# Prompt attention of a two-layer decoder on one core: the two heads of a pair walked together, value products alternating in the column halves

## The chip, the cores and the metric

One Trainium2 chip; the program runs on one of its cores. The metric is the time of one launch in microseconds (us) of device time. Engines are named as in the profile: PE is TensorE (PEld its weight loads), DVE VectorE, ACT ScalarE, POOL GpSimd, SP SyncE, whose queue only issues transfers here. The profile is of one execution.

## The reference, cut to what matters

One inference step of a decoder trunk with two layers, in fp32: a prompt of 256 tokens and 8 sample tokens, width 1024, 16 heads of 64, an MLP of width 4096 behind each mixer. The change touches the prompt's attention of both layers.

Layer 0 is a dilated sliding-window attention with three groups of keys (window, dilation: (128, 1), (512, 4), (2048, 16)). For each head and query the softmax runs in each group and the outputs are merged by the denominators, which is one softmax over all keys of the three groups:

```python
def mixer_a_prompt(h, w_in, w_out, table):
    ...
        for g, (window, dil) in enumerate(DIL_PATTERNS):
            qb = lax.dynamic_slice_in_dim(qs[g], q0, A_Q_BLOCK, axis=1)
            o, l = dilated_group(qb, ks[g], vs[g], q_idx, window, dil, table)
            outs.append(o)
            lses.append(l)
        return merge_by_denominator(outs, lses)
```

Layer 1 is a sparse attention with three branches (15 compressed keys, selected blocks, a sliding window), each with its own softmax, and their outputs added with sigmoid gates; 16 query heads share 4 key and value heads. A T5 relative bias is added to the logits of every branch in both layers.

## The kernel before

The 256 prompt tokens lie in two query tiles of 128. A unit `u` is one head and one query tile: `h, qt = u // 2, u % 2`, so the order is the small tile of a head (keys 0 to 127), then its big tile (keys 0 to 255), then the next head. There are 32 units in each layer. I call the prompt attention of layer 0 stage a and that of layer 1 stage b.

A unit of stage a passes through these steps, each on its engine, joined by semaphores:

- PE, `score_a` (L655 to L664): three products (one for each group of keys) of the queries with the keys, 64 rows deep, since a head has 64 values. The 64 rows are the lower or the upper half of the partitions by the head's parity. One fp32 product is two matmul instructions in the profile. The results lie in bank 0 (small) or banks 1 and 2 (big).
- DVE, `logits_a` (L1209 to L1224): scale, plus a mix of bias and mask, which POOL makes once a head (L540 to L547) in one of two buffers, `mixes[h % 2]`. The mix of head h waits until the logits of the units up to 2h-3 are read.
- DVE, `max_a` (L1226): maximum. ACT, `exp_a` (L1699): exponential with its sum. DVE, `diag_of` (L1195 to L1201): a diagonal matrix with the reciprocal of the sum, waiting for ACT's sum.
- PE, `turn_probs` (L699 to L710): the probabilities, in pieces of 128 columns, times the diagonal, which turns and normalises them: 3 pieces in a small unit, 6 in a big one. Results in bank 3 (small) or 4 and 5 (big). ACT, `pt_a` (L1745 to L1751) copies them out into one of two buffers, `PT`.
- PE, `pv_a` (L712 to L721): value products, 64 columns of weights each, in one column half of bank 6 or 7, 3 or 6 of them. DVE, `evac_o` (L1188): evicts the 64 x 128 result.

The orders are written out by hand. PE's loop (L732 to L745) issues for each u: scores of u+2, turn of u, value products of u-1. DVE's (L1267 to L1285): logits of u, diagonal of u-1, maximum of u, eviction of u-3, and at u = 5 and 9 a merge of the samples' outputs, `mix_a` (L1206 and L1207). ACT's: exponential of u, copy of u-1. Behind the last head's mix POOL adds the last mask to the whole bias (L549), loads a table and adds two weights (L554).

Stage b has the same shape (`score_b` L892, `pv_b` L951, PE's loop L966; `logits_b` L1394, `max_b` L1408, `rc_of` L1385, DVE's loop L1484; ACT's loop L1835). A unit has one product over 15 compressed keys and two over 128 or 256; its three sums are handled together, and POOL makes the three diagonals (L561 to L568), which wait for `rc_of`. Turned pieces: 1 of 15 rows and 2 or 4 of 128. Value products: L959 (15 rows) and L962.

SyncE's queue carries weights (L500), copies of the caches to the outputs (L452) and, between the two, the loads of layer 1's pages: `cmp_loads` (L402 to L414), which for the first sample waits for the last logits of stage a. POOL issues its own `cmp_loads` behind L554. Layer 1's projection in front of stage b (`tile`, banks 0 and 1, the last ones 7 and 6) issues the first scores between its last tiles.

## Time and profile before

| | us |
|---|---|
| median of 3 runs | 1675.91 |
| lowest, highest | 1675.38, 1677.29 |
| the profiled execution's own time | 1680.73 |
| its span | 1679.0 |
| stage a in it | 376.7 to 507.7 |
| stage b in it | 1131.1 to 1241.8 |

The mean clock that was granted to PE in this execution is 0.964 of full speed. The profiled execution stood 0.29% over the median. A group in the timeline is a run of instructions of one line on one engine: when it started, how long it was busy, the line, the operation, output and inputs, the count, and in brackets the idle time before it with what ended that. Its busy time has the end of the last instruction in it, so groups on PE overlap by some 0.1 us, and start to start is the measure of a period. A few matmul records can be missing, so that a count is 11 where 12 ran.

### The profile page before, as it was taken

How to read it: one execution, taken by the hardware profiler on the slowest of the kernel's cores; microseconds unless marked ns; L12 is line 12 of the kernel's file. 1: busy time of each engine (PE TensorE's matmuls, PEld its weight loads, DVE VectorE, ACT ScalarE, POOL GpSimd, SP SyncE). 2: the span in 40 equal slices, each digit the busy share in tenths (PEclk: the TensorE clock that was granted, in tenths of full speed). 3: DMA queues.
4: the chain of work that ended last, by engine and by line, in shares of the span. 5: the costliest groups of instructions: out<-in, count | busy, mean ns of one | idle time of the engine just before them, and what ended most of it. 6: DMA issues, size and time to landing. Idle time of an engine off the chain costs nothing.

```text
span 1679.0 us, 23479 instructions
## 1 busy us (share of the span) xinstructions
PE 1579.3 (94%) x8609; PEld 1279.6 (76%) x8609; DVE 663.4 (40%) x1533; ACT 387.4 (23%) x1166; POOL 203.4 (12%) x301
## 2 busy tenths in 40 slices
PE   6999998999989999999999999999997778999998
PEld 5877787766878878887888887886764446888886
DVE  2246512118872321003576674326546552322001
ACT  1011111113431000002566663115533220000000
POOL 1100000012230200001111120005532320000000
PEclk8799999999999999999999999999989898999999
DMA  5499999999959998787799991419966877998740
GB/s 183 158 356 383 410 401 360 337 373 355 330 164 249 284 363 299 272 292 135 128 140 140 149 186 38 122 61 352 343 200 220 285 266 242 386 372 304 276 146 31
DMA packets 170979, 423.34 MB, mean 252 GB/s; under 512 B 10400, under 2 KB 131560, under 8 KB 168064
## 3 DMA queue, kind: packets, MB, share of 16 engines
q1 hardware_dynamic: 147840, 344.27, 62.6%
q0 software_dynamic: 19312, 67.47, 15.1%
q10 hardware_dynamic: 3728, 10.32, 1.7%
q8 instruction: 58, 0.95, 0.3%
q14 instruction: 41, 0.34, 0.1%
HBM read 413.88 MB, written 192.48 MB: 361 GB/s over the span
## 4 chain that ended last, share of the span: by engine, by line
PE 82%; DMA 7%; DVE 7%; issue 2%; ACT 1%; SPq 1%; POOL 0%; ACTq 0%; DVEq 0%; POOLq 0%
PE bank L626 21%; PE bank L801 14%; PE bank L787 12%; PE bank L708 4%; PE bank L878 3%; PE bank L881 3%; PE bank L830 3%; PE bank L883 3%; DMA a_win_sample<-oT 2%; PE bank L719 2%; PE bank L663 2%; PE bank L756 1%; DMA cring<-cache_b_kv 1%; PE bank L1041 1%; DMA wring<-mlp_w_up 1%
## 5 line engine op out<-in xcount | busy, mean ns | idle before, releaser
L626 PE MATMUL bank<-hT,wring 128*128 128x264 f32 (+1 forms) x1488 | 354.0, 393 | 0.5 <-DVE area L1359 0.5
L626 PEld LDWEIGHTS bank<-hT,wring 128*128 128x128 f32 (+1 forms) x1488 | 279.2, 192 | 67.2 <-issue 8.2
L787 PE MATMUL bank<-hT,wring 128*128 128x264 f32 x1024 | 230.1, 388 | 1.9 <-DMA wring<-mlp_w_up 1.9
L801 PE MATMUL bank<-area,wring 128*128 128x264 f32 x1024 | 229.2, 386 | 2.8 <-DVE area L1312 2.8
L787 PEld LDWEIGHTS bank<-hT,wring 128*128 128x128 f32 x1024 | 195.6, 191 | 36.1 <-issue 2.3
L801 PEld LDWEIGHTS bank<-area,wring 128*128 128x128 f32 x1024 | 194.1, 190 | 37.2 <-DVE area L1310 3.6
L1689 ACT ACTIVATE turned<-xT 128x264 f32<-128x264 f32 x40 | 16.9, 423 | 548.1 <-DVE xT L1316 463.1
L1316 DVE TENSOR_TENSOR xT<-bank,xT 128x264 f32<-128x264 f32 x16 | 6.9, 432 | 224.6 <-PE bank L801 224.6
L1310 DVE SCALAR_TENSOR_TENSOR area<-bank,rv 128x264 f32 x64 | 27.7, 432 | 163.0 <-PE bank L787 162.3
L567 POOL TENSOR_SCALAR area<-ident,small 128x128 f32<-128x128 f32 x96 | 56.3, 603 | 179.4 <-DVE small L1392 179.4
L1242 DVE TENSOR_TENSOR area<-bank,rv 128x264 f32<-128x264 f32 x48 | 20.8, 432 | 106.0 <-PE bank L626 106.0
L626 PE MATMUL bank<-oT,wring 128*128 128x264 f32 x256 | 61.5, 398 | 0.9 <-DVE oT L1656 0.5
L529 POOL DMA_DIRECT2D cring<-cache_a_win x24 | 17.6, 734 | 339.4 <-PE bank L651 154.5
L626 PEld LDWEIGHTS bank<-oT,wring 128*128 128x128 f32 x256 | 50.1, 197 | 10.3 <-DVE oT L1656 0.8
L414 POOL DMA_DIRECT2D area<-cache_b_kv x32 | 17.0, 531 | 282.6 <-issue 282.6
L1242 DVE TENSOR_TENSOR oT<-bank,rv 128x264 f32<-128x264 f32 x24 | 10.4, 432 | 92.5 <-PE bank L626 92.5
L708 PE MATMUL bank<-hT,turned 128*128 128x128 f32 x240 | 36.4, 304 | 9.1 <-DVE hT L1201 8.8
L708 PE MATMUL bank<-area,turned 128*128 128x128 f32 (+1 forms) x256 | 39.9, 287 | 4.7 <-POOL area L567 3.2
L708 PEld LDWEIGHTS bank<-hT,turned 128*128 128x128 f32 x240 | 31.8, 209 | 15.6 <-issue 15.3
L708 PEld LDWEIGHTS bank<-area,turned 128*128 128x128 f32 (+1 forms) x256 | 27.6, 166 | 19.4 <-issue 18.4
L1840 ACT ACTIVATE turned<-turned,small 128x15 f32<-128x15 f32 (+2 forms) x96 | 37.8, 395 | 19.4 <-DVE small L1418 19.4
L1201 DVE SCALAR_TENSOR_TENSOR hT<-ident,small 128x128 f32<-128x128 f32 x32 | 39.8, 1244 | 1.1
(325 smaller groups left out, 2330.7 us busy)
## 6 DMA issues: line engine op xcount, KB each, us to landing
a_win_sample<-cache_a_win SPq DMA_DIRECT2D x64, 2047.0 KB, 19.5
wring<-a_w_in SPq DMA_DIRECT2D x36, 1024.0 KB, 13.0
wring<-mlp_w_up SPq DMA_DIRECT2D x32, 1024.0 KB, 10.8
wring<-mlp_w_down SPq DMA_DIRECT2D x32, 1024.0 KB, 5.3
a_win_sample<-cache_a_win SPq DMA_DIRECT2D x16, 2044.0 KB, 19.0
cring<-cache_a_win POOLq DMA_DIRECT2D x24, 1024.0 KB, 11.9
cring<-cache_b_kv POOLq DMA_DIRECT2D x62, 256.0 KB, 6.3
cring<-cache_b_kv SPq DMA_DIRECT2D x50, 256.0 KB, 7.7
```

The costliest lines, as they stand in the source:

```text
L567: ins = nc.gpsimd.tensor_scalar(diag_b[:, u % 2, k, :], ident[:, :], rc2[:, 3 * (u % 4) + k:3 * (u % 4) + k + 1], None, ALU.mult)
L626: mm = pe.matmul(bk[half if bank is None else bank][0:width, 0:R], wring[:, blk % NW, c, half * P:half * P + width], rhs[:, c, :], start=( ...
L663: mm = pe.matmul(out, qT[q0:q0 + HD, g, c, qt * P:(qt + 1) * P], kT[q0:q0 + HD, g, c, 0:n], start=True, stop=True)
L708: mm = pe.matmul(b[0:w, (j % 4) * P:(j % 4 + 1) * P], src[:, at_:at_ + w], diags[j], start=True, stop=True)
L787: mm = pe.matmul(bk[half][:, 0:R], wring[:, blk % NW, c, half * P:(half + 1) * P], hT[:, c, :], start=(c == 0), stop=(c == DC - 1))
L801: mm = pe.matmul(bk[half][:, 0:R], wring[:, blk % NW, c, half * P:(half + 1) * P], upT[:, f * R:(f + 1) * R], start=(f == 0), stop=(f == F ...
L830: mm = pe.transpose(bk[2 + h][:, i * P:(i + 1) * P], src[:, h, 2 * v + i // 2, k, (i % 2) * P:(i % 2 + 1) * P], ident[:, :])
L878: pe.matmul(accs[1][:, 0:256], wab[:, k, v + 4 * f, :], x[:, f, 1], start=(v + f == 0), stop=(v + f == 4))
L881: pe.matmul(accs[0][:, 0:256], w1[:, k, 0, v + 4 * f, :], d1[:, f], start=(v + f == 0), stop=(v + f == 4))
L883: mm = pe.matmul(accs[2][:, 0:252], w1[:, k, 1, v + 4 * f, :], d2[:, f, :, 0:63], start=(v + f == 0), stop=(v + f == 4))
L1201: dve.scalar_tensor_tensor(diag_a[:, u % 2, :], ident[:, :], rc2[:, u % 4:u % 4 + 1], ident[:, :], ALU.mult, ALU.mult).then_inc(S["diag_re ...
L1840: ins = nc.scalar.activation(L[:, a:a + w], L[:, a:a + w], ACT.Exp, bias=mx2[:, o + k:o + k + 1], accum_out=sm2[:, o + k:o + k + 1])
```

## The change

Both prompt attentions walk the heads in pairs. The order of units is now small tile of the even head, small tile of the odd head, big tile of the even, big tile of the odd (`unit(u)`). Scores get one of four places (`score_banks`). The value products run once for each pair and tile, `pv_a(w)` and `pv_b(w)`: the products of the two heads alternate, each in its column half of bank 7. One eviction of 128 x 128 takes both. So PE's loop issues value products at every second u, u even, for the two units u-2 and u-1.

Buffers follow: four mixes and four buffers for the turned probabilities where there were two of each. The mixes of heads 4 and up wait for the logits of the pair two before. The turned pieces of the small units lie in banks 3 and 4 by parity, the fifth and sixth piece of a big unit in bank 5, in its left half for the even head and in its right half for the odd; the latter waits for the copy of the unit before. The copy of a unit waits for the value products of two pairs and tiles before. The first `cmp_loads` wait for the last value products of stage a instead of its last logits. The wait for `rows_evac` 71 in front of the first scores is gone, and the wait for `oa_copied` stands in front of the scores of unit 3. The last tiles of layer 1's projection lie in banks 7 and 5.

```diff
--- before.py
+++ after.py
@@ -188,7 +188,7 @@
-        mixes = (cring[:, 0, 2048:2816], cring[:, 0, 3072:3840])
+        mixes = (cring[:, 0, 2048:2816], cring[:, 0, 3072:3840], cring[:, 1, 2304:3072], cring[:, 1, 3072:3840])
...
@@ -204,8 +204,8 @@
-        LG = (turned_f[:, 1536:1920], turned_f[:, 0:768], small[:, 128:512], turned_f[:, 768:1536])
-        PT = hT_f[:, 0:2 * 768].rearrange("p (i n) -> p i n", i=2)
+        LG = (turned_f[:, 1536:1920], small[:, 128:512], turned_f[:, 0:768], turned_f[:, 768:1536])
+        PT = (cring[:, 1, 0:384], cring[:, 1, 384:768], cring[:, 1, 768:1536], cring[:, 1, 1536:2304])
...
@@ -251,10 +251,10 @@
-        PB = hT_f[:, 0:2 * 640].rearrange("p (i n) -> p i n", i=2)
+        PB = (hT_f[:, 0:384], hT_f[:, 384:768], hT_f[:, 768:1408], hT_f[:, 1408:2048])
...
-        LB = (turned_f[:, 0:272], turned_f[:, 544:1072], turned_f[:, 272:544], turned_f[:, 1072:1600])
+        LB = (turned_f[:, 0:272], turned_f[:, 272:544], turned_f[:, 544:1072], turned_f[:, 1072:1600])
...
@@ -303,6 +303,14 @@
+        def unit(u):
+            return 2 * (u // 4) + u % 2, u // 2 % 2
+        def score_banks(u):
+            return ((bk[0], None), (bk[1], None), (bk[2], bk[0]), (bk[1], bk[6]))[u % 4]
         def a_slot(i):
...
@@ -402,7 +410,7 @@
         def cmp_loads(eng, b, js, landed_sem):
...
-                eng.wait_ge(S["logits_read"], 2 * H)
+                eng.wait_ge(S["pv_done"], 2 * H)
...
@@ -541,9 +549,11 @@
                     for i in range(NA, 2 * NK):
...
-                if h >= 2:
-                    pool.wait_ge(S["logits_read"], 2 * h - 2)
-                nc.gpsimd.tensor_tensor(mixes[h % 2].rearrange("p (g k) -> p g k", g=NG), bias[:, h, :].unsqueeze(1).broadcast_to([P, NG, 2 * P]),
+                if h in (2, 3):
+                    pool.wait_ge(S["pva_done"], 12)
+                if h >= 4:
+                    pool.wait_ge(S["logits_read"], 4 * (h // 2 - 2) + 3 + h % 2)
+                nc.gpsimd.tensor_tensor(mixes[h % 4].rearrange("p (g k) -> p g k", g=NG), bias[:, h, :].unsqueeze(1).broadcast_to([P, NG, 2 * P]),
...
@@ -653,13 +663,14 @@
             def score_a(u):
-                h, qt = u // 2, u % 2
+                h, qt = unit(u)
...
+                b, b2 = score_banks(u)
                 for g in range(NG):
-                    out = bk[0][:, g * P:(g + 1) * P] if qt == 0 else (bk[1][:, g * 256:(g + 1) * 256] if g < 2 else bk[2][:, 0:256])
+                    out = b[:, g * n:(g + 1) * n] if g < 2 or qt == 0 else b2[:, 0:256]
...
@@ -702,25 +713,28 @@
                     pe.wait_ge(S["pt_ready"], u[0] - 1)
                 pe.wait_ge(S["probs_ready"], u[0] + 1)
                 pe.wait_ge(S["diag_ready"], u[0] + 1)
-                at_ = 0
+                at_, e = 0, u[1] % 2
                 for j, w in enumerate(widths):
-                    b = bk[3] if u[1] % 2 == 0 else bk[4 + j // 4]
-                    mm = pe.matmul(b[0:w, (j % 4) * P:(j % 4 + 1) * P], src[:, at_:at_ + w], diags[j], start=True, stop=True)
+                    if j == 4 and e:
+                        pe.wait_ge(S["pt_ready"], u[0])
+                    b, o = (bk[3 + e], j * P) if j < 4 else (bk[5], 256 * e + (j - 4) * P)
+                    mm = pe.matmul(b[0:w, o:o + P], src[:, at_:at_ + w], diags[j], start=True, stop=True)
                     at_ += max(w, 16)
                 mm.then_inc(S["probs_turned"], 1)
-            def pv_a(u):
-                h, qt = u // 2, u % 2
-                pe.wait_ge(S["pt_ready"], u + 1)
-                if u >= 2:
-                    pe.wait_ge(S["o_evac"], u - 1)
-                n, e = qt + 1, h % 2
+            def pv_a(w):
+                c, qt = w // 2, w % 2
+                pe.wait_ge(S["pt_ready"], 2 * w + 2)
+                if w:
+                    pe.wait_ge(S["o_evac"], 2 * w)
+                n = qt + 1
                 for j in range(NG * n):
-                    mm = pe.matmul(bk[6 + u % 2][64 * e:64 * e + 64, 0:P], V[:, j % n, j // n, h * HD:(h + 1) * HD], PT[:, u % 2, j * P:(j + 1) * P],
-                                   start=(j == 0), stop=(j == NG * n - 1))
-                mm.then_inc(S["pv_done"], 1)
-            pe.wait_ge(S["rows_evac"], 71)
+                    for e in range(2):
+                        h = 2 * c + e
+                        mm = pe.matmul(bk[7][64 * e:64 * e + 64, 0:P], V[:, j % n, j // n, h * HD:(h + 1) * HD], PT[2 * qt + e][:, j * P:(j + 1) * P],
+                                       start=(j == 0), stop=(j == NG * n - 1))
+                mm.then_inc(S["pv_done"], 2)
             score_a(1)
             pe.wait_ge(S["rows_evac"], 72)
             for i in range(2 * NS):
@@ -730,19 +744,20 @@
             for u in range(2 * H):
+                if u == 1:
+                    pe.wait_ge(S["oa_copied"], 1)
...
-                n = NG * (u % 2 + 1)
-                if u == 1:
-                    pe.wait_ge(S["oa_copied"], 1)
+                n = NG * (unit(u)[1] + 1)
...
-                if u:
-                    pv_a(u - 1)
+                if u and u % 2 == 0:
+                    pv_a(u // 2 - 1)
...
+            pe.wait_ge(S["pt_ready"], 2 * H - 1)
             for st in range(NS):
...
-            pv_a(2 * H - 1)
+            pv_a(H - 1)
             def turn(n):
...
@@ -915,7 +931,7 @@
-                    tile(blk, half, E_BIN + p, hT, P if j != 6 else 48, p % 2 if p < 19 else 26 - p).then_inc(S["gemm_done"], 1 if j != 6 else 2)
+                    tile(blk, half, E_BIN + p, hT, P if j != 6 else 48, p % 2 if p < 19 else 45 - 2 * p).then_inc(S["gemm_done"], 1 if j != 6 else 2)
...
@@ -948,29 +964,29 @@
             pe.wait_ge(S["gates_ready"], 2)
-            def pv_b(u):
-                h, qt = u // 2, u % 2
-                g, n = h // KVH, qt + 1
-                pe.wait_ge(S["pt_ready"], U0 + u + 1)
-                if u >= 2:
-                    pe.wait_ge(S["o_evac"], U0 + u - 1)
-                e = h % 2
-                o, pt = bk[6 + u % 2][64 * e:64 * e + 64, 0:P], PB[:, u % 2, :]
-                pe.matmul(o, vcP[0:CMP, g * HD:(g + 1) * HD], pt[0:CMP, 0:P], start=True, stop=False)
+            def pv_b(w):
+                c, qt = w // 2, w % 2
+                g, n = c // 2, qt + 1
+                pe.wait_ge(S["pt_ready"], U0 + 2 * w + 2)
+                if w:
+                    pe.wait_ge(S["o_evac"], U0 + 2 * w)
+                for e in range(2):
+                    pe.matmul(bk[7][64 * e:64 * e + 64, 0:P], vcP[0:CMP, g * HD:(g + 1) * HD], PB[2 * qt + e][0:CMP, 0:P], start=True, stop=False)
                 for k in range(2):
                     for j in range(n):
-                        mm = pe.matmul(o, kvrow[:, j, (3 + 2 * k) * GW + g * HD:(3 + 2 * k) * GW + (g + 1) * HD],
-                                       pt[:, (1 + k * n + j) * P:(2 + k * n + j) * P], start=False, stop=(k == 1 and j == n - 1))
-                mm.then_inc(S["pv_done"], 1)
+                        for e in range(2):
+                            mm = pe.matmul(bk[7][64 * e:64 * e + 64, 0:P], kvrow[:, j, (3 + 2 * k) * GW + g * HD:(3 + 2 * k) * GW + (g + 1) * HD],
+                                           PB[2 * qt + e][:, (1 + k * n + j) * P:(2 + k * n + j) * P], start=False, stop=(k == 1 and j == n - 1))
+                mm.then_inc(S["pv_done"], 2)
             for u in range(2 * H):
                 if 4 <= u + 2 < 2 * H:
                     score_b(u + 2)
-                n = u % 2 + 1
+                n = unit(u)[1] + 1
                 turn_probs((U0 + u, u), [CMP] + [P] * (2 * n), LB[u % 4], [diag_b[:, u % 2, 0, :]] + [diag_b[:, u % 2, 1, :]] * n + [diag_b[:, u % 2, 2, :]] * n)
-                if u:
-                    pv_b(u - 1)
-            pv_b(2 * H - 1)
+                if u and u % 2 == 0:
+                    pv_b(u // 2 - 1)
+            pv_b(H - 1)
             pe.wait_ge(S["o_evac"], 4 * H)
@@ -1185,12 +1201,10 @@
-            def evac_o(first, u):
-                h, qt = u // 2, u % 2
-                e = h % 2
-                dve.wait_ge(S["pv_done"], first + u + 1)
-                dve.tensor_copy(oT[64 * e:64 * e + 64, h // 2, qt * P:(qt + 1) * P], bk[6 + u % 2][64 * e:64 * e + 64, 0:P]).then_inc(S["o_evac"], 1)
+            def evac_o(first, w):
+                dve.wait_ge(S["pv_done"], first + 2 * w + 2)
+                dve.tensor_copy(oT[:, w // 2, w % 2 * P:(w % 2 + 1) * P], bk[7][:, 0:P]).then_inc(S["o_evac"], 2)
             def diag_of(u):
...
@@ -1269,20 +1284,19 @@
-                if u >= 3:
-                    evac_o(0, u - 3)
+                if u >= 4 and u % 2 == 0:
+                    evac_o(0, u // 2 - 2)
...
-            evac_o(0, 2 * H - 3)
-            evac_o(0, 2 * H - 2)
+            evac_o(0, H - 2)
...
             for st in range(NS):
                 for e in range(2):
...
-            evac_o(0, 2 * H - 1)
+            evac_o(0, H - 1)
             def square(n):
...
@@ -1429,7 +1444,7 @@
-                src = bk[i % 2 if i < 19 else 26 - i][:, 0:R]
+                src = bk[i % 2 if i < 19 else 45 - 2 * i][:, 0:R]
...
@@ -1742,16 +1757,15 @@
-            def copy_pt(u, parts_cols, PTb):
+            def pt_a(u):
+                e = u % 2
+                parts = [(3 + e, 0, 384, 0)] if u // 2 % 2 == 0 else [(3 + e, 0, 512, 0), (5, 256 * e, 256, 512)]
...
-                if u >= 2:
-                    act.wait_ge(S["pv_done"], u - 1)
-                for parts, bank, c0, n, o in parts_cols:
-                    ins = nc.scalar.copy(PTb[0:parts, o:o + n], bk[bank][0:parts, c0:c0 + n])
+                if u >= 4:
+                    act.wait_ge(S["pv_done"], 2 * (u // 2 - 1))
+                for bank, c0, n, o in parts:
+                    ins = nc.scalar.copy(PT[u % 4][:, o:o + n], bk[bank][:, c0:c0 + n])
...
-            def pt_a(u):
-                copy_pt(u, [(P, 3, 0, 384, 0)] if u % 2 == 0 else [(P, 4, 0, 512, 0), (P, 5, 0, 256, 512)], PT[:, u % 2, :])
             for u in range(2 * H):
...
@@ -1823,18 +1837,19 @@
             def pt_b(u):
-                parts = ([(CMP, 3, 0, P, 0), (P, 3, P, 256, P)] if u % 2 == 0 else
-                         [(CMP, 4, 0, P, 0), (P, 4, P, 384, P), (P, 5, 0, P, 512)])
+                e = u % 2
+                parts = ([(CMP, 3 + e, 0, P, 0), (P, 3 + e, P, 256, P)] if u // 2 % 2 == 0 else
+                         [(CMP, 3 + e, 0, P, 0), (P, 3 + e, P, 384, P), (P, 5, 256 * e, P, 512)])
...
-                if u >= 2:
-                    act.wait_ge(S["pv_done"], U0 + u - 1)
+                if u >= 4:
+                    act.wait_ge(S["pv_done"], U0 + 2 * (u // 2 - 1))
                 for np_, bank, c0, n, o in parts:
-                    ins = nc.scalar.copy(PB[0:np_, u % 2, o:o + n], bk[bank][0:np_, c0:c0 + n])
+                    ins = nc.scalar.copy(PB[u % 4][0:np_, o:o + n], bk[bank][0:np_, c0:c0 + n])
...
             for u in range(2 * H):
...
-                n = (u % 2 + 1) * P
+                n = (u // 2 % 2 + 1) * P
...
                 for k, (a, w) in enumerate(((0, CMP), (16, n), (16 + n, n))):
...
```

## Rows read from the trace of the kernel before

**Rows 1.** The page, part 1: busy time of each engine.

```profile
PE 1579.3 (94%) x8609; PEld 1279.6 (76%) x8609; DVE 663.4 (40%) x1533; ACT 387.4 (23%) x1166; POOL 203.4 (12%) x301
```

**Rows 2.** Windows: length, busy PE, PEld, DVE, ACT, POOL, granted clock, DMA share, GB/s.

```profile
376.70:507.70 131.00, 121.20 (x797) 98.71 (x796) 103.21 (x182) 49.44 (x116) 34.74 (x16) 0.95 0.86 279
1131.10:1241.80 110.70, 106.00 (x682) 76.49 (x682) 62.21 (x278) 58.08 (x260) 52.81 (x90) 1.00 0.96 323
426.00:440.20 14.20, 14.10 (x98) 11.72 (x97) 11.35 (x22) 5.51 (x14) 3.62 (x2) 1.00 1.04 338
1176.60:1190.50 13.90, 13.73 (x90) 9.93 (x89) 8.11 (x36) 7.60 (x34) 7.04 (x12) 1.00 0.98 355
```

**Rows 3.** Timeline of a steady head of stage a, PE, DVE and POOL.

```profile
438.68 1.52 PE L719 MATMUL bank<-hT,area 128*64 128x128 f32 x12
...
440.13 1.56 PE L663 MATMUL bank<-area 64*128 64x256 f32 x6
...
441.62 1.60 PE L708 MATMUL bank<-hT,turned 128*128 128x128 f32 x12
...
442.83 1.82 POOL L546 TENSOR_TENSOR cring<-bias,mprompt 128x768 f32<-128x768 f32 x1 [5.28 <-DVE turned L1223]
442.85 1.94 DVE L1201 SCALAR_TENSOR_TENSOR hT<-ident,small 128x128 f32<-128x128 f32 x1
...
443.15 0.87 PE L719 MATMUL bank<-hT,area 128*64 128x128 f32 x6
...
443.95 0.93 PE L663 MATMUL bank<-area 64*128 64x128 f32 x6
...
444.94 0.91 PE L708 MATMUL bank<-hT,turned 128*128 128x128 f32 x6
```

**Rows 4.** Timeline of a big unit of stage b, PE, DVE and POOL.

```profile
1181.29 0.39 PE L899 MATMUL bank<-area 64*128 64x15 f32 x2
...
1182.57 1.48 PE L708 MATMUL bank<-area,turned 128*15 128x128 f32 x10
...
1184.02 1.76 POOL L567 TENSOR_SCALAR area<-ident,small 128x128 f32<-128x128 f32 x3 [2.27 <-DVE small L1392]
...
1185.93 1.02 PE L708 MATMUL bank<-area,turned 128*15 128x128 f32 x6
```

**Rows 5.** Timeline, PE: products in two column halves, and full-width ones.

```profile
817.63 0.65 PE L839 MATMUL bank<-oT,area 128*64 128x254 f32 x4
...
1004.08 1.03 PE L881 MATMUL bank<-turned,area 128*128 128x256 f32 x4
```

**Rows 6.** Timeline and windows: pauses of PE, and the granted clock around them.

```profile
397.19 1.23 DVE L1206 TENSOR_TENSOR cring<-cring,cb 128x1024 f32<-128x1024 f32 x1
...
398.45 1.90 DVE L1207 TENSOR_REDUCE area<-cring 128x64 f32<-128x1024 f32 x1
...
401.54 2.57 PE L708 MATMUL bank<-hT,turned 128*128 128x128 f32 x12 [1.57 <-DVE hT L1201]
...
489.32 2.90 PE L708 MATMUL bank<-hT,turned 128*128 128x128 f32 x12 [5.06 <-DVE hT L1201]
...
659.58 2.71 PE L801 MATMUL bank<-area,wring 128*128 128x264 f32 x11 [1.39 <-DVE area L1312]
...
401.90:405.30 3.40, 3.40 (x17) 3.06 (x16) 3.33 (x6) 1.56 (x4) 1.81 (x1) 0.50 1.00 344
655.50:659.50 4.00, 2.69 (x13) 1.94 (x11) 1.05 (x3) 0.00 (x0) 0.00 (x0) 1.00 0.83 331
```

**Rows 7.** Timeline: the second turn of stage b.

```profile
1136.47 1.02 PE L708 MATMUL bank<-area,turned 128*15 128x128 f32 x6 [1.03 <-POOL area L567]
```

**Rows 8.** Windows: a stretch behind stage b.

```profile
1250.50:1255.50 5.00, 5.00 (x21) 3.54 (x14) 0.00 (x0) 0.89 (x2) 0.00 (x0) 0.50 0.02 4
```

**Rows 9.** Timeline of SyncE's queue behind stage a; waits from 507 to 700.

```profile
500.72 10.08 SPq L414 DMA_DIRECT2D cring<-cache_b_kv  x8
...
PE bank L787 <- DMA wring<-mlp_w_up: 1.9, 1, 1.9
```

41 lines of the change are left out of this document (22 added, 19 removed).

## The prediction

> **What bounds the kernel now.** I began with the busy table: TensorE (PE) is busy 94% of the span [rows 1], at a mean granted clock of 0.964. Read alone, that says that PE work taken out is time taken out. The change touches two stages, so I went on to the windows: layer 0's prompt attention (stage a) takes 131.0 us and layer 1's (stage b) 110.7 [rows 2]. One steady pair of heads keeps PE busy 14.10 of 14.20 us in a and 13.73 of 13.90 in b [rows 2]. That looks PE-bound, but the timeline shows a tie. In a, PE's groups follow each other start to start as big scores 1.49, big turn (L708, x12) 1.53, small value products (L719) 0.80, small scores 0.96, small turn 0.84, big value products 1.45: 7.07 a head [rows 3]. Beside it runs a loop of waits of the same length: scores 1.56, logits on VectorE (DVE) that bring the diagonal to 442.85, and the diagonal, 1.94 instead of 0.35, because GpSimd's (POOL's) mix of 1.82 starts with it, released by the same logits [rows 3]; then the small turn that needs the diagonal. From the big scores' start to the small turn's are 4.8 us, and 0.84 + 1.45 more close the head. Stage b has the same shape: 6.97 a head, half of the window of a pair (scores 1.28 from row to row, and 0.99, turns 1.41 and 0.98, value products 0.93 and 1.38), with POOL making the diagonals in 1.76 each [rows 4]; from the big scores' start (1181.29, with the compressed keys) to the turn that waits for what they led to (1185.93) are 4.64 us.
>
> **The value products.** A pair's two heads had a run of products each, now they alternate between column halves. The trace has one group of that form: L839, four matmuls of 254 columns in 0.65 us, against 1.03 for four of 256 columns in full width at L881 [rows 5]. So two halves stream beside each other. I cost a pair's run as one head's now: 0.80 + 1.45 saved a pair in a, 0.93 + 1.38 in b, 2.3 us each. Bounds: nothing saved at all, or this.
>
> The Trainium skill, page "TensorE: Matmul & The Clock Gate", section "The mechanism", says that a weight load overlaps running matmuls only where the row groups differ. Here all share the same 128 rows, and by that rule each load would be bare. The trace is against it: L719's twelve loads and matmuls take 1.52 us [rows 3], with nothing left over for bare loads. It is kept as a rival below.
>
> **What takes the place of that work.** The new order is small, small, big, big for each pair. I follow stage a's chain at full clock from one first big turn to the next: 0.13 + big turn 1.53, small products 0.80, small scores 0.96, second big turn 1.53, big scores 1.60; then DVE alone: logits 0.93, diagonal 2.05 (still beside a mix, since both mixes of a pair are now released by the logits of its big units), max 0.95, eviction 0.27, logits 0.93, diagonal 2.05. That is 13.73 us a pair against 14.20, though PE has only 2 x (1.49 + 1.53 + 0.96 + 0.84) + 2.25 = 11.89 of work. The rest, 1.84 us, is a pause in front of the first big turn of a pair: there PE has scores, a small turn and scores (3.29) to do while that turn's diagonal is 5.13 us off. Eight pairs save some 4 us; DVE's two extra merges (L1206 and L1207, 1.23 + 1.90 [rows 6]) now fall partly in the pauses and cost about 1.6 each instead of 3.1, 3 more. At full clock, stage a would give 7.3 us back.
>
> Stage b at full clock: PE work of a pair is 2 x 6.97 - 2.31 = 11.63. The first big turn comes 4.64 us after the second big scores start (2.73 to the diagonals' start, 1.76 of them, 0.15 of hand-over [rows 4]), and only 1.28 + 0.98 + 0.96 of work lies between: a pause of 1.42, and one of 0.28 ahead of the small turn (its diagonals, by the same steps from the small scores). 13.33 a pair against 13.94, some 5 us over the stage. At its start it is worse: the turn at 1136.47 waited 1.03 us for POOL [rows 7]. In the new order it is a big turn, released no earlier, and the small value products (0.93) now come behind it, a big turn ahead has become a small one (0.43), and a hand-over of some 0.3 is gone as well: about 2.7 us of pause.
>
> **The clock.** The change trades a PE that never stops for one that stops in every pair. What the trace shows of that [rows 6]: after the pause of 1.57 us that ended at 401.54, the stretch from 401.9 to 405.3 ran at granted 0.50, the lower level of 1.2 GHz. After 5.06 us in front of 489.32 the same twelve turns took 2.90 instead of 1.60. In 655.5 to 659.5 there was a pause of 1.39 (ended at 659.58) and the clock stayed at 1.00 (2.4 GHz), as it did around the 1.03 in stage b [rows 7, 2]. The new pauses of 1.84 are longer than one that was followed by half clock; that of 2.7 far longer. So I take the clock as lost in a after some five of eight pauses, and surely at the start of b.
>
> Its price in a: 3.40 us of solid work at half clock [rows 6] is 1.7 us of work lost, five or six times, some 9.3. Stage a: -7.3 + 9.3 = **+2**. It comes back there, as it did after 405.3 in before: full-height work is dense.
>
> In b, does it come back? There a score group feeds 64 rows, compressed products 15. The nearest row is L1006's neighbourhood: PE busy 5.00 of 5.00 us with 8-row products, and granted 0.50 throughout [rows 8]. Busy time alone doesn't bring the clock back. I take b between these: once lost it stays lost. Price: the twelve matmuls of L708 went from 1.60 [rows 3] to 2.90 [rows 6], 0.108 us more for each 128 columns. A pair of b streams 32 such in turns, 24 in scores (256 columns counting twice), and 16 in value products: 72 x 0.108 = 7.8, 19.4 us a pair. It is then bound by PE; the pauses vanish. From the first big turn at about 1136.8 to the last pair's are 7 x 19.4 = 135.8, 1272.6; two turns of 2.48, products of 1.57 and 2.45 and the eviction, 9.4: 1282.0, where before came to 1241.8. Stage b: **+40**.
>
> **The rest.** The first page loads of layer 1's cache on SyncE's queue (10.08 us of issue at 500.72 [rows 9]) wait for the last value product instead of the last logits, some 7 us later relative to it. Behind them lie weight loads; PE's one wait on these, 1.9 us [rows 9], may grow by 0 to 2: +0.5. Bank 5, shared by the two big units, makes the odd one's fifth piece wait for the copy of the even one (0.86 at the longest): PE has other groups of some 3 us between the two turns, 0; without that cover 0.86 a pair. Mixes in four buffers: released by the same kind of logits, 0. The eviction for both heads moves 128 partitions instead of 64 in the same 0.27: 16 of 32 go in each stage, off the path. The second projection's bank order, the small scores' banks and the removed wait at the start of a: 0. Copies of turned probabilities wait for value products two units older: covered, 0.
>
> **Sum.** +2 + 40 + 0.5 = +42.5 on the profiled execution's 1680.7 is 1723.2; it stood 4.8 (0.29%) over the median of 1675.9, so **1718** for the median. A measurement of this kernel tells about 0.2%, 3.4 us, from no change.
>
> **The rivals.**
> - Forecast, b at half clock throughout: 1700 to 1727 (with a between -4 and +8, and b's pair 18.5 to 19.8). Chance 0.56.
> - The clock comes back in b between pauses: each pair pays one to two stretches of 1.7 and gains 0.61, 8 x (1.7 to 3.4) - 5 = +9 to +22, with a's +2: 1684 to 1700. For it: stage a in before did come back. 0.15.
> - The clock holds, the other side: pauses of 1.84 leave it at 2.4 GHz in both stages. -7.3 - 5 + 1 = 1665, **faster**. It decides in front of the first big turn of b, at 1136.8: granted 1.00 behind it, and b ends before 1240. For it: 1.39 was borne. Against it: 1.57 wasn't. 0.15. The Trainium skill's same page, section "Why this matters for your kernels", warns only of idle gaps longer than any of these; by that rule the new pauses are harmless and 1665 comes out. The trace disagrees, with the half clock behind 1.57 us.
> - The chain is shorter than I think and PE alone counts: 2.3 a pair in both stages, 16 pairs, 1638. Against: 5.13 from rows. 0.03.
> - The halves don't stream together: a pair in a is 13.73 + 0.80, in b about 15.1, with few pauses left: +2.6 - 3 + 9 = 1684. Against: L839. 0.04.
> - Weight loads stay bare between alternating halves: at most 0.33 a run in a and 0.9 a pair in b: 1675 with the clock held, 1730 with it lost. 0.04.
> - The later loads hold up the MLP's weights just enough to meet the gain, with the clock held: 1673 to 1679. 0.03.
>
> Range: 1668 to 1730; what it leaves out is the clock held (0.15) and PE alone (0.03). Faster by over 0.2%: these two, 0.18. Within: the late loads and half of the bare ones, 0.05. Slower: the rest, 0.77.
>
> **What would show it.** Right: L719 and L962 as groups of x24 and x12 with twice as many matmuls in the same 1.4 to 1.5 us; one pause of 1.8 a pair in a before the first big turn; granted clock of b near 0.5 and its pairs 19 us apart. Wrong: granted 1.00 throughout b (then b is 5 us shorter); value runs of 2.5 us (no overlap); the diagonal at 0.35 in big units (the mix not beside it); PE's wait for MLP weights over 4 us.

## The result, and the profile after

The changed kernel took 1730.21 us (median of 4 runs, 1714.69 to 1738.99), against 1675.64 for the kernel before beside it: a ratio of 1.0325, 95% interval 1.0243 to 1.0408, slower. The forecast was 1718, range 1668 to 1730. The direction and the mechanism came as forecast; stage b's part of it was a quarter larger, and the median lies 0.2 us above the range. Some executions come out longer than the rest, 31 of the 77 of the kernel before that ran beside the experiments, all but one of them by 20 to 80 us, and the ratios leave out, of every kernel, what lies over 1.5% above its fastest execution, while medians count all.

The profiled execution took 1727.76 us, with a span of 1726.0, 47.0 over the one before. The page's busy and clock lines [rows 1]:

```profile
PE 1616.7 (94%) x8609; PEld 1302.7 (75%) x8609; DVE 648.5 (38%) x1501; ACT 385.4 (22%) x1166; POOL 203.4 (12%) x301
...
PEclk8899999998899999998999999965558898999999
```

PE is busy for the same share, with the same number of instructions, and 37 us longer. The clock line has three slices of 5 and one of 6 where it had three of 9 and one of 8. The windows (length, busy PE, PEld, DVE, ACT, POOL, granted clock, DMA share, GB/s) of stage a, of stage b and of one pair of b [rows 2]:

```profile
384.50:504.80 120.30, 102.25 (x753) 85.19 (x752) 92.48 (x162) 46.77 (x112) 31.09 (x14) 0.89 0.83 275
1126.10:1287.60 161.50, 155.78 (x682) 110.26 (x682) 57.42 (x261) 56.87 (x260) 52.81 (x90) 0.52 0.65 221
1152.33:1173.08 20.75, 20.72 (x88) 14.70 (x89) 7.55 (x34) 7.38 (x35) 7.04 (x12) 0.50 0.98 320
```

A pair of b is 20.75 us of unbroken PE work at 0.50. From its first turn to the product behind it, b takes 161.5 us where it took 110.6 (1131.20 to 1241.77 before). The whole account: stage a ends at 504.81 instead of 507.73, -2.9; the stretch between a and b is 2.2 shorter; b +50.9; what lies behind b +1.2. Together 47.0.

The timeline of PE around b's start [rows 7], of the same kernel, and of one pair:

```profile
1126.08 2.00 PE L721 MATMUL bank<-area,turned 128*15 128x128 f32 x12 [0.52 <-DVE area L1449]
...
1131.57 2.59 PE L721 MATMUL bank<-area,turned 128*15 128x128 f32 x10 [2.63 <-POOL area L577]
...
1152.33 2.59 PE L721 MATMUL bank<-area,turned 128*15 128x128 f32 x10
1154.85 0.69 PE L974 MATMUL bank<-hT,area 15*64 15x128 f32 x4
1155.47 1.12 PE L978 MATMUL bank<-hT,area 128*64 128x128 f32 x8
1156.52 0.61 PE L915 MATMUL bank<-area 64*128 64x15 f32 x2
1156.97 1.20 PE L917 MATMUL bank<-area 64*128 64x128 f32 x4
1158.10 2.61 PE L721 MATMUL bank<-area,turned 128*15 128x128 f32 x10
1160.64 0.61 PE L915 MATMUL bank<-area 64*128 64x15 f32 x2
1161.09 2.05 PE L917 MATMUL bank<-area 64*128 64x256 f32 x4
1163.07 1.76 PE L721 MATMUL bank<-area,turned 128*15 128x128 f32 x6
...
1276.85 2.59 PE L721 MATMUL bank<-area,turned 128*15 128x128 f32 x10 [1.60 <-POOL area L577]
```

The pause of 2.63 us stands where it was forecast with 2.7, and the first ten turns behind it take 2.59 instead of 1.48 [rows 4]. Then no group waits until the last pair, whose first big turn waits 1.60 us (1276.85) and whose last value products wait 0.87. In stage a the same view shows a value run for both heads (L734) and then, for five of the eight pairs, the pause in front of the first big turn and what followed it:

```profile
403.04 1.53 PE L734 MATMUL bank<-cring,area 128*64 128x128 f32 x24
...
409.51 1.58 PE L721 MATMUL bank<-hT,turned 128*128 128x128 f32 x12 [1.72 <-DVE hT L1215]
...
424.50 2.49 PE L721 MATMUL bank<-hT,turned 128*128 128x128 f32 x12 [2.25 <-DVE hT L1215]
...
439.62 1.58 PE L721 MATMUL bank<-hT,turned 128*128 128x128 f32 x12 [1.72 <-DVE hT L1215]
...
453.14 1.58 PE L721 MATMUL bank<-hT,turned 128*128 128x128 f32 x12 [1.72 <-DVE hT L1215]
...
466.68 2.90 PE L721 MATMUL bank<-hT,turned 128*128 128x128 f32 x12 [1.72 <-DVE hT L1215]
```

Pairs are 13.5 us apart (439.62, 453.14, 466.68), against 14.2 before. The pause was 1.72 us four times; three times the twelve turns behind it took 1.58 us (full clock) and once 2.90 (half), so the length of a pause doesn't say which.

### The profile page after: what moved, and what is told of

It is laid out like the page before. It is cut to its first block, busy times and chain, and to the rows that moved or that the text cites. A ratio compares the mean times of both kernels' runs of the same rounds, so it can differ in the third digit from the quotient of the medians.

```text
span 1726.0 us, 23447 instructions
## 1 busy us (share of the span) xinstructions
PE 1616.7 (94%) x8609; PEld 1302.7 (75%) x8609; DVE 648.5 (38%) x1501; ACT 385.4 (22%) x1166; POOL 203.4 (12%) x301
## 4 chain that ended last, share of the span: by engine, by line
PE 84%; DVE 7%; DMA 5%; issue 2%; ACT 1%; SPq 0%; POOL 0%; ACTq 0%; DVEq 0%; POOLq 0%
PE bank L636 21%; PE bank L816 13%; PE bank L802 12%; PE bank L721 5%; PE bank L893 3%; PE bank L896 3%; PE bank L845 3%; PE bank L898 3%; PE bank L917 2%; DMA a_win_sample<-oT 2%; DMA wring<-mlp_w_up 1%; PE bank L771 1%; PE bank L1057 1%; PE bank L978 1%; DMA a_win_sample<-area 1%
## 5 line engine op out<-in xcount | busy, mean ns | idle before, releaser
L721 PE MATMUL bank<-area,turned 128*128 128x128 f32 (+1 forms) x256 | 68.3, 430 | 4.9 <-POOL area L577 4.2
L721 PEld LDWEIGHTS bank<-area,turned 128*128 128x128 f32 (+1 forms) x256 | 46.6, 266 | 31.2 <-issue 30.2
L917 PE MATMUL bank<-area 64*128 64x256 f32 (+1 forms) x128 | 47.3, 527 | 0.0
L1847 ACT COPY hT<-bank 15x128 f32<-15x128 f32 (+2 forms) x80 | 20.8, 316 | 106.6 <-PE bank L721 106.6
```

Of the source, the lines that this page charges most:

```text
L721: mm = pe.matmul(b[0:w, o:o + P], src[:, at_:at_ + w], diags[j], start=True, stop=True)
L917: mm = pe.matmul(b[:, o + k * n:o + (k + 1) * n], q, kD[q0:q0 + HD, k, g, 0:n], start=True, stop=True)
```

## The experiments

In all kernels that fill pauses, the filler is this function, whose products nobody reads:

```diff
+            def fill(n):
+                for _ in range(n):
+                    pe.matmul(bk[2][:, 0:P], ident[:, :], ident[:, :], start=True, stop=True)
```

In each comparison the median in brackets is that of all executions of the kernel before beside it; "b" is stage b from its first turn to the product behind it, in the traced execution.

**Is it the pause at b's start, the pauses in its pairs, or the halves?** Four kernels on one chip (before: 1684.15).

```diff
                 n = unit(u)[1] + 1
+                if u == 2:
+                    fill(12)
                 turn_probs((U0 + u, u), ...
```

> The changed kernel, with twelve products of the identity with itself (full height, 128 columns, into bank 2, read by nobody) put into the pause of 2.63 us in front of stage b's first big turn, and nowhere else. Theory (the pause at the start loses the clock and b's light work never wins it back): granted clock of b near 1.00, pairs of 13.3 us with pauses of 1.4 in place of 20.75, b some 50 us shorter, the whole near 1680. Second theory (b's new mix of work with 1.4 us pauses loses the clock again by itself): the clock holds for one or more pairs, then 0.5 for the rest; the whole 1690 to 1720. Rival (the alternating halves, not the pauses, pull the clock down): 0.5 from the first value products on, the whole stays near 1730.

1720.76 us, ratio 1.0265 (1.0201 to 1.0329). Windows of b, first the start, then the stretch up to 1182, then the rest:

```profile
1132.70:1145.00 12.30, 11.65 (x86) 9.15 (x86) 7.27 (x36) 6.71 (x31) 4.54 (x8) 1.00 1.15 417
1145.00:1155.00 10.00, 7.64 (x48) 5.51 (x49) 4.47 (x20) 4.39 (x20) 4.26 (x8) 0.83 0.99 321
1155.00:1182.00 27.00, 23.39 (x178) 16.95 (x178) 15.53 (x72) 15.01 (x68) 14.09 (x25) 0.97 0.96 315
1182.00:1274.00 92.00, 89.44 (x396) 63.55 (x395) 29.98 (x134) 31.09 (x142) 29.91 (x51) 0.50 0.60 206
```

The second theory's case: the start is borne, the clock dips behind a pause of 1.51 us at 1145.9, comes back, bears two pauses of 1.47 (at 1154.4 and 1167.7), and goes behind a third of 1.47, at 1181, until the end of b. b takes 142.0 us in this trace, so the start pause alone isn't the whole of it. The halves run at 1.00 for 12 us, so they don't pull it down.

```diff
+                if u % 4 == 2:
+                    fill(12 if u == 2 else 6)
                 turn_probs((U0 + u, u), ...
```

> As the run before it, and six such products in front of the first big turn of every pair of stage b (1.3 us, as long as the pause). Theory: the clock is 1.00 through all of b, its pair 13.3 us, the whole near 1680. If the pauses of 1.4 matter, this run is faster than the one that fills only the start; if they don't, the same within 3 us. Rival (alternating halves): near 1730 or above, since the fillers then cost 2.6 us a pair at half clock.

1676.45, ratio 1.0008 (0.9967 to 1.0048): 44 us less than with the start alone, for six products a pair that fill the pause. One dip of some 10 us was left, from 1142 to 1152, and b took 111.8 us.

```diff
                 n = NG * (unit(u)[1] + 1)
+                if u > 2 and u % 4 == 2:
+                    fill(8)
                 turn_probs((u, u), ...
```

> As the run before it, and eight such products (1.7 us) in front of each pair's first big turn in stage a too. Theory: no half clock in a but behind the mask's 8.8 us addition, 2 to 3 windows of half clock saved at 1.5 us each: 3 to 5 us faster than the run before it, near 1676. Rival (in a the DVE chain hides what the half clock costs): the same within 2 us.

1671.44, ratio 0.9974 (0.9940 to 1.0008). In its trace b is at 1.00 from end to end and takes 107.1 us, its pairs 13.30 apart (1177.23, 1190.53), which is the full-clock sum of the forecast (13.33):

```profile
1130.50:1237.50 107.00, 100.76 (x788) 76.12 (x788) 57.55 (x261) 57.69 (x260) 52.82 (x90) 1.00 0.98 334
...
1178.64 0.44 PE L981 MATMUL bank<-hT,area 15*64 15x128 f32 x4
1179.00 0.66 PE L985 MATMUL bank<-hT,area 128*64 128x128 f32 x8
1179.59 0.39 PE L922 MATMUL bank<-area 64*128 64x15 f32 x2
```

A small value run for both heads takes 0.95 us start to start at full clock (1178.64 to 1179.59), against the 0.93 of one head before. Stage a took 122.15 us here and between 119.9 and 126.8 in the five traces whose stage a is the change's own, so this run can't tell what the filling of a is worth.

The fourth kernel takes back the alternation alone:

```diff
-                for j in range(NG * n):
-                    for e in range(2):
+                for e in range(2):
+                    for j in range(NG * n):
...
```

> The changed kernel with the alternation alone undone: in each value run the products of the even head come first, then those of the odd head, in the same two column halves, with the same order of units, buffers and single eviction. That puts back 2.3 us of PE work a pair. Theory (pauses lose the clock): in a the pair is 14.5 us, the pause in front of the first big turn stays near 1.8 since none of the work lies there; in b the start pause of 2.6 stays, so b still goes to half clock and takes 2.3 to 4.6 us more a pair: the whole 1750 to 1770. Rival (alternating halves pull the clock down): b at 1.00, 1685 or less. Second rival (the halves don't stream beside each other, so that the order is indifferent): same as the changed kernel, 1730.

1759.19, ratio 1.0486 (1.0403 to 1.0569), as the theory had it: b 186.7 us at a mean clock of 0.56, 25 more than with alternation. A pair of b at half clock, and a big value run of a at full clock, all with the halves in turn:

```profile
447.30 2.46 PE L734 MATMUL bank<-cring,area 128*64 128x128 f32 x24
...
1142.36 2.59 PE L721 MATMUL bank<-area,turned 128*15 128x128 f32 x10 [2.63 <-POOL area L577]
...
1156.44 0.69 PE L974 MATMUL bank<-hT,area 15*64 15x128 f32 x2
...
1161.47 0.61 PE L915 MATMUL bank<-area 64*128 64x15 f32 x2
...
1167.26 2.59 PE L721 MATMUL bank<-area,turned 128*15 128x128 f32 x10
```

The pair takes 24.90 us (1142.36 to 1167.26) where it took 20.75, and the big value run 5.03 (1156.44 to 1161.47) where it took 2.53. So the halves do stream beside each other when they alternate, at half clock too. In a the same 24 matmuls take 2.46 us in turn and 1.53 alternated; a small run takes 1.07 in turn (start to start), less than the 2 x 0.80 of two separate runs before. So in a some of the 2.25 us that a pair saves comes from joining the two heads' runs, and the alternation itself is worth 1.20; in b it is worth the whole 2.3.

**Shorter chains in place of fillers, and the old kernel with a pause.** Four kernels (before: 1681.90).

```diff
-                dve.tensor_tensor(rc, rc, grow[:, qt, h, :], ALU.mult).then_inc(S["rc_ready"], 1)
+                link(dve.tensor_tensor(rc, rc, grow[:, qt, h, :], ALU.mult))
...
+                dve.tensor_tensor(diag_b[:, u % 2], ident[:, :].unsqueeze(1).broadcast_to([P, 3, P]), rc.unsqueeze(2).broadcast_to([P, 3, P]), ALU.mult)...
```

> The changed kernel, with stage b's three diagonals of a unit made by one VectorE instruction (identity times the three reciprocals, 128 x 384) right behind the reciprocals, in place of three GpSimd instructions of 1.76 us together. No filler. An estimate from DVE's rows of that size: 0.4 to 0.6 us. Theory (pauses of over about 1.5 us in a row of light work lose the clock): the start pause falls from 2.63 to some 1.3 and the pause in each pair from 1.4 to near 0, the clock holds at 1.00, a pair takes 11.7 to 12.5 us in place of 13.3: b about 95 to 102 us, the whole 1663 to 1672. Rival (the start pause is still too long): b at half clock, DVE faster or not: 1725 to 1731, since b is bound by PE there.

(The loop of three GpSimd instructions is taken out.) 1701.44, ratio 1.0131 (1.0041 to 1.0221): neither. The diagonals take 0.56 us, and the pauses shrink (1.37 at the start), but b alternates between the levels (1.00 in 1161 to 1179 and 1231 to 1250, 0.50 in 1141 to 1155 and 1186 to 1224) and takes 126.8.

```diff
-                dve.scalar_tensor_tensor(diag_a[:, u % 2, :], ident[:, :], rc2[:, u % 4:u % 4 + 1], ident[:, :], ALU.mult, ALU.mult)...
+                nc.scalar.mul(diag_a[:, u % 2, :], ident[:, :], rc2[:, u % 4:u % 4 + 1]).then_inc(S["diag_ready"], 1)
```

> As the run before it, and stage a's diagonals made on ScalarE (identity times the reciprocal) instead of VectorE, so that no diagonal stands beside a GpSimd mix. Theory: the pause in front of the first big turn of a pair in a goes from 1.84 to 0.1 to 0.5, a's pair from 13.7 to 12.0 to 12.4 us, no half clock in a: 12 to 20 us less than the run before it if the clock holds in b in both. Rival (ScalarE takes the place of the diagonal in the chain, or VectorE's other instructions now collide with the mix): a gains less than 5 us.

1680.65 with runs from 1657.87 to 1702.02, ratio 0.9930 (0.9863 to 0.9997). Stage a, which took 125.1 us before and 120.3 after, takes 95.0:

```profile
385.60:480.60 95.00, 91.63 (x753) 76.04 (x753) 58.05 (x129) 55.96 (x141) 31.28 (x14) 1.00 1.01 339
1099.60:1243.70 144.10, 137.98 (x680) 98.14 (x680) 74.42 (x290) 57.40 (x260) 0.00 (x0) 0.60 0.73 248
...
444.83 1.83 POOL L556 TENSOR_TENSOR cring<-bias,mprompt 128x768 f32<-128x768 f32 x1 [6.28 <-DVE turned L1229]
444.97 0.40 ACT L1769 ACTIVATE hT<-ident,small 128x128 f32<-128x128 f32 x1
```

The diagonal takes 0.40 us on ScalarE beside a mix of 1.83 that made it 1.94 on VectorE [rows 3]. But b is still at 0.60 on average. The clock goes behind the second of two pauses of 1.37 and 1.31 us at its start, and from 1130 to 1170 PE is busy without a pause and stays at 0.50:

```profile
1111.32 1.18 PE L715 MATMUL bank<-area,turned 128*15 128x128 f32 x6 [1.31 <-DVE area L1400]
```

The ratio counts only the five shortest of its ten executions; the medians of all, 1680.65 against 1681.90, show no gain from stage a's 25 us, since b gives them back (144.2 us in this trace).

```diff
--- before.py
+                if u == 2:
+                    for k in range(3):
+                        nc.gpsimd.tensor_scalar(diag_b[:, 0, k, :], ident[:, :], 0.0, None, ALU.mult)...
...
                 for k in range(3):
```

> The kernel before, with nothing of the change in it: three more GpSimd instructions of 0.6 us, writing zeros to a diagonal's buffer that is overwritten at once, in front of the diagonals of unit 2 of stage b. They lengthen the pause that PE has at 1136.5 from 1.03 to about 2.9 us, once. Theory (a pause of that length at the start of b loses the clock, and b's work never wins it back, whatever the order or the halves): granted clock 0.5 through the rest of b, b some 60 us longer, the whole 1730 to 1745. Rival (the order of units or the halves are needed for the loss): b 1.9 us longer, the whole 1676 to 1690.

1696.70 (1678.67 to 1731.18), too scattered for a ratio. Its trace shows both theory and rival short of the mark:

```profile
1135.06 1.02 PE L712 MATMUL bank<-area,turned 128*15 128x128 f32 x6 [2.66 <-POOL area L571]
...
1128.20:1136.00 7.80, 5.14 (x34) 3.65 (x34) 3.65 (x16) 3.65 (x17) 4.38 (x8) 1.00 1.13 405
1138.00:1162.00 24.00, 24.00 (x86) 16.69 (x85) 9.63 (x45) 6.78 (x32) 6.97 (x12) 0.50 1.00 325
1165.00:1250.00 85.00, 82.56 (x532) 59.72 (x531) 47.54 (x210) 45.19 (x201) 42.45 (x72) 1.00 0.81 272
```

The clock went behind the longer pause in the old order too; there it came back after 24 us, and b took 123.7 us, 13 more than before.

```diff
+                if u == 2:
+                    fill(6)
```

> As the run with both diagonals moved, and six filler products (1.3 us) in front of the first big turn of stage b, once. If the start pause of some 1.3 us did no harm without them: the same within 2 us. If the run without them is at half clock in b, this one is 50 us faster: near 1650 to 1660.

1687.63 (1663.81 to 1705.24), ratio 1.0021 (0.9975 to 1.0067), against 1680.65 without: no gain from filling the start pause once the chains are short. The second pause, 1.31 us at 1111.5, was left, and b was at 0.50 for some 60 us from there on.

**Fillers and short chains together, and what belongs to which.** Four kernels (before: 1681.09).

```diff
+                if u % 4 == 2:
+                    fill(12 if u == 2 else 6)
```

> The kernel with both diagonals moved (a's to ScalarE, b's to one VectorE instruction), with twelve filler products in front of stage b's first big turn and six in front of the first big turn of each later pair. Theory (the fillers are what kept the clock in the kernel with all pauses of b filled): b at 1.00 throughout, its pair 12.8 to 13.2 us, b 103 to 108 us, a 95 us as in the run without fillers: the whole 1635 to 1645, faster than the kernel before and than every run so far. Rival (the clock falls in b anyway, since there are fewer pauses to fill and the work is light): b 125 or more, 1660 or above.

1649.73, ratio 0.9843 (0.9781 to 0.9904). b at 1.00 up to its last products, 104.7 us.

```diff
-                    fill(12 if u == 2 else 6)
+                    fill(12 if u == 2 else 3)
```

> The same with three fillers a pair in b instead of six. Theory: if half as much dense work is enough, b's pair is 12.3 us, 4 to 5 us faster than with six. If it isn't, b goes to half clock for some pairs, and this run is 10 to 40 us slower than with six, with a wider scatter from run to run.

1646.31 (1641.26 to 1649.82), ratio 0.9821 (0.9760 to 0.9881), the fastest kernel of the study, though the interval overlaps that of the one with six; its four runs lie within 8.6 us. Stage a and b of its trace, and a pair of a:

```profile
383.30:484.50 101.20, 97.89 (x753) 81.25 (x753) 58.27 (x130) 55.80 (x141) 31.28 (x14) 0.93 0.96 326
1109.70:1213.50 103.80, 96.75 (x746) 71.62 (x746) 73.40 (x291) 56.07 (x260) 0.00 (x0) 1.00 0.99 342
...
441.31 1.58 PE L720 MATMUL bank<-hT,turned 128*128 128x128 f32 x12
...
453.22 1.58 PE L720 MATMUL bank<-hT,turned 128*128 128x128 f32 x12
```

A pair of a takes 11.91 us, the PE work that the forecast counted (11.89). Stage a took 95.0 us in two of the traces with the short chain and 99.6 and 101.2 in the two others, which start it at half clock.

The kernel before with ScalarE's diagonals in a and nothing else (the edit of the sixth kernel, in the old order):

> The kernel before with stage a's diagonals on ScalarE and nothing else. Theory (in before PE's work of 7.07 a head and the chain stood level, so that a shorter chain alone gives little): the steady pair stays at 14.1 us; what goes are the stops behind the 8.8 us addition and half of the two merges, with their half clock: a 10 to 13 us shorter, 112 to 115 in place of 125, the whole 1662 to 1668. Rival (the chain alone was the bound): a 100 us or less, and then the change's paired value products brought nothing in a.

1672.27 (1659.40 to 1736.16), ratio 0.9977 (0.9933 to 1.0021). Stage a 113.9 us, its steady pair still 14.2: without the paired values the short chain gives only what the stops cost. Its traced execution, one of 1712.13, also shows what a long run of the old order is:

```profile
426.00:440.20 14.20, 14.20 (x100) 11.90 (x99) 7.65 (x19) 7.08 (x20) 3.64 (x2) 1.00 1.08 361
1130.00:1245.00 115.00, 115.00 (x406) 80.87 (x407) 37.65 (x166) 32.88 (x153) 31.70 (x54) 0.50 0.76 257
...
1119.47 1.02 PE L708 MATMUL bank<-area,turned 128*15 128x128 f32 x6 [1.03 <-POOL area L567]
...
1127.11 1.02 PE L708 MATMUL bank<-area,turned 128*15 128x128 f32 x6 [0.76 <-POOL area L567]
...
1128.42 1.58 PE L962 MATMUL bank<-hT,area 128*64 128x128 f32 x8
```

Stage b is the old order's own here, with the pause of 1.03 of [rows 7]. Behind two pauses, 1.03 and 0.76, the clock is gone for 115 us, and b takes 162.9 us, as long as the changed kernel's 161.5. The profiled execution of the kernel before had the same two pauses, 1.03 at 1136.47 and this one, and kept the clock:

```profile
1144.11 1.02 PE L708 MATMUL bank<-area,turned 128*15 128x128 f32 x6 [0.75 <-POOL area L567]
```

So these pauses don't decide by themselves whether the clock goes; no run here shows what else does.

```diff
+                if u > 2 and u % 4 == 2:
+                    fill(6)
```

> The changed kernel with six fillers in front of the first big turn of every pair of b but the first, so that the start pause of 2.63 us stays. Theory (the clock, once lost, stays lost because too little of b's work is dense): the clock falls at the start as in the changed kernel, the dense fillers let it come back after one to three pairs, and it holds from there: b 120 to 140 us, the whole 1690 to 1705. Rival (at half clock nothing in b brings it back): b at 0.50 throughout, each pair longer by the fillers' 2.6 us: 1745 to 1750.

1679.43 (1672.97 to 1688.67), ratio 1.0018 (0.9975 to 1.0061). The mechanism as the theory had it, 10 us better than its number:

```profile
1134.00:1156.00 22.00, 22.00 (x95) 15.94 (x95) 9.05 (x43) 7.38 (x34) 7.56 (x13) 0.50 0.97 334
1160.00:1240.00 80.00, 76.17 (x590) 57.05 (x588) 43.31 (x193) 44.30 (x200) 42.16 (x72) 1.00 0.87 295
```

The clock goes behind the start pause, is back after 22 us with fillers in it, and stays. Against the changed kernel that is seven times six products more, and some 50 us less (1.0018 against 1.0325).

**What was still open.** Two kernels (before: 1681.62).

```diff
--- before.py
+                if u == 2:
+                    pe.wait_ge(S["pt_ready"], U0 + 1)
+                    for _ in range(6):
+                        pe.matmul(bk[3][:, 0:P], ident[:, :], ident[:, :], start=True, stop=True)
                 turn_probs((U0 + u, u), ...
```

> The kernel before with six filler products (identity with itself, into bank 3, overwritten by the next turn) in the pause of 1.03 us in front of unit 2's turn in stage b, and nothing else. Theory (that pause decides whether the old order keeps the clock in b, and in two of five executions it doesn't): all runs within 1665 to 1685, while the kernel before beside it scatters up to 1740. Rival (the clock is lost in b at other places, or for another reason): the same scatter with the fillers as without, some runs over 1700.

1680.08, ratio 0.9995 (0.9951 to 1.0039). In its trace the pause is filled and b takes 111.0 us. Two of 10 runs lay over 1695 (1728.43, and 2048.72, far outside the rest), against 8 of 20 for the kernel before beside it (one of them, 2529.94, as far outside). That leans to the theory and settles nothing.

> The kernel with both diagonals moved and three fillers a pair in b, with the alternation undone in both value runs (even head's products first, then the odd head's). Theory (with the clock held and short chains PE's work is what counts, and alternating saves 2.25 us a pair in a and 2.31 in b, less what fits into the remaining pauses): 25 to 36 us slower than with alternation, 1672 to 1683. Rival (the halves' gain is hidden in pauses): less than 10 us slower.

(The edit is that of the fourth kernel, on the fastest one.) 1671.52 (1663.83 to 1674.56), ratio 0.9959 (0.9935 to 0.9983). Between 0.9959 and 0.9821 lie 1.4%, 23 us: the worth of the alternating halves once the clock is held, a little under the expected range. In its trace b takes 116.1 us at 1.00, 12.3 more than with alternation, and a 107.2, 6.1 more; the expectation took the whole 2.25 us a pair of a for the alternation's, of which it is 1.20.

## Why the prediction missed, step by step

**The value products: right.** 0.95 us and 1.39 (1184.49 to 1185.88) for both heads in b at full clock, forecast 0.93 and 1.38; in a, 0.80 and 1.46. The Trainium skill's rule that loads overlap running matmuls only where the row groups differ (page "TensorE: Matmul & The Clock Gate", section "The mechanism") doesn't hold for this form: all share the same 128 rows, and the 24 loads of a run of L734 hide in the 1.53 us that the 12 matmuls of one head took. The same section also lets a load go ahead into a background weight buffer; no run here shows whether that is what happens.

**The chain and its pauses: right.** In a 1.72 us (forecast 1.84) and pairs of 13.5 (13.73); in b 2.63 at the start (2.7), 1.47 in a pair that nothing filled (1.42), and 13.30 a pair with the clock held (13.33).

**The clock in a: right in kind, too often.** The forecast took five of eight pauses to be followed by half clock and +2 us for the stage. There were six such pauses, of 1.72 to 2.25 us, and three were followed by half clock (391.63, 424.50, 466.68); the turn behind a further pause of 2.98, beside the large mask addition (475.61), ran at half clock too. The stage ended 2.9 earlier.

**The clock in b, "once lost it stays lost": right for this kernel's trace, mis-sized.** This is the step that failed: stage b was put at +40 and measured +50.9. The price of half clock was counted as streamed columns alone, 72 x 0.108 us, 19.4 a pair. The pair took 20.75. What the sum had nothing for are the four groups of scores over 15 compressed keys, which stream hardly any columns. Each took 0.45 us start to start (1160.64 to 1161.09) where it had taken 0.24, as these rows of before show:

```profile
1181.29 0.39 PE L899 MATMUL bank<-area 64*128 64x15 f32 x2
1181.53 1.11 PE L901 MATMUL bank<-area 64*128 64x256 f32 x4
```

That is 0.8 of the missing 1.35. The rest is spread over the other groups: big turns took 2.52 to 2.54 (2.48 in the sum), value runs 1.67 and 2.53 (1.57 and 2.45), and the other scores some 0.2 more in all. So there is a part of each group that doesn't go by its columns and is dearer at half clock too. Seven times 1.35 are 9.4 of the missing 10.9; the rest is in the end of the stage, where two waits of 1.60 and 0.87 us stand.

**How far the number was off.** In the profiled execution the forecast missed by 4.6 us (1727.76 against 1723.2): 10.9 too little in b, 4.9 too much in a, and 1.5 too much elsewhere. That the errors partly cancel is luck. The rest of the 12.2 between 1718 and 1730.21 comes from the step from the trace to the median: before, the profiled execution stood 4.8 over its median, and this was taken off; here it stood 2.5 under. Two of the four runs lie inside the range.

**A premise that says less than it was used for.** The clock "stayed at 1.00 (2.4 GHz), as it did around the 1.03 in stage b" is what the trace of before shows, and the forecast took it for the way of the old kernel. The traced execution of the old stage b at 0.50 has the same pauses. That an order stays at half clock isn't a property of b's work alone either: it came back after 24 us in the old order, and after 22 with fillers, and in the changed kernel's trace not in the 156 us from the pause to the end of b. Why it didn't come back there was not isolated. One reason would be that alternation halves the value runs, since without it the clock was back for some 7 us at 1186; but with alternation and without fillers in the pairs it also came back, after a dip of 5 us in the first kernel and by 1161 in the one with the short chain in b alone. So that reason is not shown.

**The rival of the held clock** (1665, chance 0.15) is what the kernel with both stages filled comes near to: ratio 0.9974 (0.9940 to 1.0008), where 1665 would be 0.9935. The Trainium skill's rule for it (same page, section "Why this matters for your kernels") isn't borne out: half clock began behind pauses of 1.72 in a, and of 0.76 in the old b, both far shorter than the gaps it warns of.

**The rest.** PE's wait for the MLP's weights grew from 1.9 to 4.2 us (forecast 0 to 2 more). That is over the 4 us that the forecast had named as a sign of being wrong, and yet the stretch between a and b became 2.2 us shorter; one wait of 2.0 for the page loads is gone from it.

**Sums.** Three sums of the prediction don't come out: stage a's gain at full clock is 4 and 3, so 7 and not 7.3; the rival with the clock coming back begins at 1687 and not at 1684; and the forecast's own terms give some 1706 and not 1700 at the lower end. None of them changes the forecast by more than 0.3 us.

## What to carry to other kernels

Taking work out of a busy TensorE makes pauses, and here what followed the pauses cost more than the work was worth: sum the chain first, and where it doesn't shrink with the work, shorten it (the diagonals' move took 19 to 25 us out of stage a) before the work is cut. Where a stage's products are small and light, a few full-height products in a pause that exists anyway can be the cheapest fix: three a pair, with the chain shortened, kept a whole stage at 2.4 GHz in the trace. Whether they work by closing the pause or by the full-height work that they add was not separated: every filler here did both, and the kernel with short chains and few pauses was still at 0.60. Judge a kernel that runs near the edge by many executions, since one trace may show either level.

## What the runs showed of the hardware

Half clock in b lasted 22 and 24 us in two traces, some 60 in two with short chains, 92 and 115 in two others, and 156 in the changed kernel, with hardly a pause of PE in any of them: PE was busy 152.9 of those 156 us at a granted 0.50. In a, pauses of the same 1.72 us were followed by full clock three times and by half clock once; in the old b, pauses of 1.03 and 0.75 or 0.76 by full clock in one trace and by half clock in another. VectorE's 128 x 128 diagonal takes 1.94 us instead of 0.35 beside GpSimd's mix, ScalarE's takes 0.40. Products that alternate in two column halves run at the pace of one head's, at 2.4 GHz and at 1.2 GHz too: a big run of b takes 2.53 us alternated and 5.03 in turn at half clock. The score product over 15 columns costs 0.24 us start to start at 2.4 GHz and 0.45 at 1.2 GHz.
